# The first expert blocks of a hybrid decoder step: row numbers and first down weights loaded at the end of the output projection

## The reference

```
x  = x + gt1 * (concat([att, conv]) @ w_out)
h2 = rmsnorm(x, g_n2) * (1 + sc2) + sh2
x  = x + gt2 * hierarchical_moe(h2)           # top-1 of 4 groups, top-2 of 8 experts in it

def expert_mlp(xb, w1, w3, w2):               # 32 experts, w1, w3: 1024 x 512, w2: 512 x 1024
    return (silu(xb @ w1) * (xb @ w3)) @ w2
```

## Time and profile before

| what | value |
|---|---|
| median of 3 runs | 2175.88 us (2175.57 to 2178.8) |
| the profiled execution, own time | 2180.36 us |
| its span, first to last instruction | 2178.8 us |
| mean granted TensorE clock | 0.967 of full speed |
| TensorE busy | 1983.6 us, 91% of the span |
| VectorE, ScalarE, GpSimd busy | 72%, 48%, 24% |
| DMA | 553.20 MB, mean 254 GB/s |

### The profile page before, as it was taken

How to read it: one execution, slowest core, us unless ns; L and a number is a source line. 1 busy time by engine, 2 the same in 40 slices (tenths; PEclk the granted TensorE clock), 3 DMA queues, 4 the chain that set the end, 5 groups by cost and what they waited for, 6 DMA issues and landing times. The chain is left out here.

```text
span 2178.8 us, 40353 instructions
## 1 busy us (share of the span) xinstructions
PE 1983.6 (91%) x13272; PEld 1592.3 (73%) x13273; DVE 1563.6 (72%) x3053; ACT 1051.0 (48%) x2056; POOL 533.0 (24%) x571
## 2 busy tenths in 40 slices
PE   5999999998999998699999399999899998999976
PEld 3788888886787786388887378788687876778732
DVE  2648889886888887489997478565447574658757
ACT  2411111111888887244543267555536574557623
POOL 1013444331111153026554201001110101100155
PEclk9999999998999999799999599999999999999989
DMA  8787555665668578767876389974749797769968
GB/s 252 235 279 254 187 190 189 226 227 175 213 177 285 181 280 275 259 196 243 262 278 202 122 300 395 334 289 167 273 173 330 267 359 255 273 234 387 384 238 313
DMA packets 221314, 553.20 MB, mean 254 GB/s; under 512 B 28802, under 2 KB 43482, under 8 KB 219929
## 3 DMA queue, kind: packets, MB, share of 16 engines
q1 hardware_dynamic: 170891, 425.60, 56.1%
q0 software_dynamic: 25088, 75.71, 9.7%
q10 hardware_dynamic: 25239, 50.67, 6.7%
HBM read 456.95 MB, written 167.56 MB: 287 GB/s over the span
## 5 line engine op out<-in xcount | busy, mean ns | idle before, releaser
L2528 DVE TENSOR_TENSOR LO<-WIDE,HI 128x2048 fp32r<-128x2048 f32 x128 | 287.1, 2285 | 86.1 <-ACT HI L2450 86.1
L644 DVE SCALAR_TENSOR_TENSOR arena<-arena,tapw 128x512 f32<-128x512 f32 (+3 forms) x435 | 266.3, 692 | 0.0
L2450 ACT CAST HI<-WIDE 128x2048 fp32r<-128x2048 f32 x128 | 238.0, 1909 | 24.0 <-PEq L217 16.5
L2528 DVE TENSOR_TENSOR LO<-W2E,HI 128x2048 fp32r<-128x2048 f32 x64 | 143.8, 2289 | 92.8 <-ACT HI L2450 92.8
L445 POOL TENSOR_TENSOR STATS<-STATS,K 128x1 f32<-128x1 f32 x16 | 131.3, 8205 | 314.2 <-ACT H L497 314.2
L777 PE MATMUL PJ<-WIN_H,HTH 128*128 128x512 f32 x640 | 160.4, 393 | 5.3 <-ACT HTH L505 4.9
L787 PE MATMUL PJ<-WIN_L,HTH 128*128 128x512 f32 x640 | 158.7, 390 | 0.0
L781 PE MATMUL PJ<-WIN_H,HTL 128*128 128x512 f32 x640 | 158.3, 389 | 0.0
L2450 ACT CAST HI<-W2E 128x2048 fp32r<-128x2048 f32 x64 | 118.8, 1904 | 60.3 <-issue 60.3
L777 PEld LDWEIGHTS PJ<-WIN_H,HTH 128*128 128x128 f32 x640 | 118.6, 188 | 33.5 <-issue 9.0
L781 PEld LDWEIGHTS PJ<-WIN_H,HTL 128*128 128x128 f32 x640 | 120.2, 188 | 25.2
(11 more groups left out here) (366 smaller groups left out, 4500.8 us busy)
## 6 DMA issues: line engine op xcount, KB each, us to landing
WIDE<-in_w_expert_gate SPq DMA_DIRECT2D x64, 1024.0 KB, 8.2
WIDE<-in_w_expert_up SPq DMA_DIRECT2D x64, 1024.0 KB, 10.0
W2E<-in_w_expert_down SPq DMA_DIRECT2D x64, 1024.0 KB, 9.8
expert_rows<-YE ACTq DMA_DIRECT2D x40, 512.0 KB
expert_rows<-NOROWS POOLq DMA_DIRECT2D x11, 1536.0 KB, 11.7
QN<-q_rows SPq DMA_DIRECT2D x48, 256.0 KB
KN<-out_new_k_prompt SPq DMA_DIRECT2D x48, 256.0 KB, 4.9
VN<-out_new_v_prompt SPq DMA_DIRECT2D x48, 256.0 KB, 4.7
```

Of the source, the lines that this page charges most:

```text
L644: ins = nc.vector.scalar_tensor_tensor(out=out, in0=src, scalar=tap, in1=out, op0=ALU.mult, op1=ALU.add)
L2450: nc.scalar.copy(HI[n][:, cols], raw[n][:, cols]).then_inc(hi_ready[n], 1)
L2528: nc.vector.tensor_tensor(LO[n][:, cols], raw[n][:, cols], HI[n][:, cols], ALU.subtract).then_inc(lo_ready[n], 1)
```

## The change

Row numbers: SyncE's program in the output projection gets an end in which it waits for the last write to `slot` and loads the numbers of expert 0's first 32 slots and of the 128 behind them into two columns of a new lasting tile, FIRST_IDX. In the expert stage GpSimd's first two instructions gather XG0 (32 rows) and XG (128 rows) by these columns. The number load for the second small block goes from GpSimd to SyncE, at the start of SyncE's program. GpSimd then gathers that block, waits for the first 128-row block's landing and for its turn (`x_turned` at 2), and enters its loop, which is as it was: it fetches block 0 again. TensorE's first `turn_x` waits for the new gather's semaphore in place of `x_in`. Down weights: expert 0's two halves are loaded by SyncE in round 16 of the output projection; W2E is allotted one stage earlier for that.

```diff
@@ output_projection_and_routing, SyncE
                     if isinstance(i, int) and i == TILES - 1:
                         first_expert("w_expert_up", 1)
+                    if isinstance(i, int) and i == TILES:
+                        w = t["w_expert_down"][0].rearrange("e (k p) d -> e p k d", p=P)[0]
+                        for half in range(2):
+                            ks = slice(half * KF // 2, half * KF // 2 + KF // 2)
+                            sp.dma_start(state["down"][:, ks], w[:, ks]).then_inc(state["down_in"][half], 16)
...
                 sp.wait_ge(h2_out, 16 * ALLT + 16)
+                sp.wait_ge(slot_out, 16 * 2 * ALLT)
+                for n, (at, rows) in enumerate(((0, SMALL_ROWS), (SMALL_ROWS, P))):
+                    sp.dma_start(state["first_rows"][0:rows, n:n + 1], dr["slot"][at:at + rows, :]).then_inc(state["first_rows_in"][n], 16)
@@ experts, SyncE
-                sp.wait_ge(first_x_in, 16)
-                for half in range(2):
-                    sp.dma_start(half_of(W2[:], half), half_of(w2[0], half)).then_inc(w2_in[half], 16)
+                second = nc.s_assert_within(sp.snap(entry(sp, 0, 1, 1, LAST) * CAP), 0, NEXP * CAP - T,
+                                            skip_runtime_bounds_check_because="an expert's blocks stay inside its CAP slots")
+                sp.dma_start(IDXS[:], dr["slot"][ds(second, T), :]).then_inc(second_idx_in, 16)
@@ experts, GpSimd
                     pool.dma_start(IDXS[:], dr["slot"][ds(slot, T), :]).then_inc(sidx_in, 16)
-                    pool.wait_ge(sidx_in, n * 16)
+                    pool.wait_ge(sidx_in, pool.snap(n * 16 - 16))
...
-                second = place(entry(pool, 0, 1, 1, LAST) * CAP, T)
-                pool.dma_start(IDX0[:], dr["slot"][0:T, :]).then_inc(first_idx_in, 16)
-                pool.dma_start(IDXS[:], dr["slot"][ds(second, T), :]).then_inc(sidx_in, 16)
-                pool.wait_ge(first_idx_in, 16)
-                pool.indirect_dma_start(XG0[:], None, dr["h2"], bass.IndirectOffsetOnAxis(ap=IDX0[:].bitcast(U32), axis=0)).then_inc(first_x_in, 16)
-                pool.wait_ge(sidx_in, 16)
+                for n, (rows, dst, come) in enumerate(((T, XG0, first_x_in), (P, XG, first_block_in))):
+                    pool.wait_ge(state["first_rows_in"][n], 16)
+                    pool.indirect_dma_start(dst[:], None, dr["h2"], bass.IndirectOffsetOnAxis(ap=FIRST[0:rows, n:n + 1].bitcast(U32), axis=0)).then_inc(come, 16)
+                pool.wait_ge(second_idx_in, 16)
                 pool.indirect_dma_start(XGS[:], None, dr["h2"], bass.IndirectOffsetOnAxis(ap=IDXS[:].bitcast(U32), axis=0)).then_inc(sx_in, 16)
+                pool.wait_ge(first_block_in, 16)
+                pool.wait_ge(x_turned, 2)
                 with pool.Fori(0, runs(pool)) as g:
@@ experts, TensorE
-                        pe.wait_ge(x_in, 16)
+                        pe.wait_ge(first_block_in, 16)
```

More of the change, by code:

```diff
@@ L192, in decoder_step @@
             state["unit"] = persistent("unit", [P, NEXP])
+            state["first_rows"] = persistent("FIRST_IDX", [P, 16], I32)
+            state["first_rows_in"] = [lasting(f"first_idx_in{n}") for n in range(2)]
+            state["down"] = persistent("W2E", [P, KF, D])
+            state["down_in"] = [lasting(f"down_w_in{half}") for half in range(2)]
             output_projection_and_routing(nc, t, scratch, const, const_at, state)
@@ L197, in decoder_step @@
             state["mods6_in"] = lasting("mods6_in")
-            state["down"] = persistent("W2E", [P, KF, D])
             state["x6_in"] = [lasting(f"x6_early_in{n}") for n in range(3)]
@@ L2290, in experts @@
         w1_in, w3_in = state["first_in"]
-        w2_in = [sem(f"down_w_in{half}") for half in range(2)]
+        w2_in = state["down_in"]
         idx_in, x_in = sem("idx_in"), sem("xg_in")
@@ L2298, in experts @@
                                         "y_taken", "y_out"))
-        first_idx_in, first_x_in, first_turned = sem("first_idx_in"), sem("first_x_in"), sem("first_turned")
+        first_x_in, first_block_in, first_turned, second_idx_in = sem("first_x_in"), sem("first_block_in"), sem("first_turned"), sem("second_idx_in")
         table = state["blocks"]
         SEL, BASE = sb("SEL", [P, ALLT * 2, NEXP]), sb("BASE", [P, ALLT * 2])
-        IDXS, IDX0, XG0 = sb("IDXS", [T, 1], I32), sb("IDXS0", [T, 1], I32), sb("XGS0", [T, D])
+        IDXS, XG0 = sb("IDXS", [T, 1], I32), sb("XGS0", [T, D])
+        FIRST = state["first_rows"]
         step = sem("dest_step")
```

## The result

The changed kernel takes 2190.78 us (2190.47 to 2195.31, 4 runs) against 2177.34 (2175.57 to 2178.95) for the kernel before: a ratio of 1.0068, 95% interval 1.0053 to 1.0082, 13.4 us slower. The forecast was 2181 with a range of 2174.5 to 2187.

What follows compares the result with a forecast made beforehand. TensorE was taken to bound the expert loop; the first big matmul gains 8.0 us, but the second block's rows come 2.9 us late plus 2.0 of clock: 2175.9 + 4.9 = 2180.8, written 2181, range 2174.5 to 2187.

Steps and rivals of the forecast that it cites:

- The end of the output projection: SyncE's added loads before the stage's closing barrier: cost 0, hidden under GpSimd's drain, bounded by 0 and 1 us.
- the small block's gain: First small block at the expert stage's entry: rows 3 us sooner, of which ScalarE's four casts leave 0.8 us.
- The stop at the second block: TensorE waits about 11 us for the second 128-row block's rows, some 12 us behind its first big matmul.
- The sum is +2.9 + 2.0 = +4.9 us: At the second 128-row block: 2.9 us lost by late rows plus 2.0 us for TensorE's fallen clock.
- The third term: GpSimd's chain ahead of the second block: block 0's gather to landing 5.5 us, then 3.5 to the next number load.
- The step that failed: Expert loop: bound by TensorE, so a stall inside it moves the end by as much.
- The fourth rival: Row chain stays the bound in the loop: fetch cycle over TensorE's, further stalls, 2185 to 2192 us; chance 0.08.
- the upper bound of the forecast's sum, +13.5: Second block with all chain terms near the top: 11.0 us late plus 2.5 of clock, called unlikely.
- Quiet queues: Rival: both index loads and gathers run at least times, second block on time, 2174.5 to 2178 us; chance 0.33.
- The rule of about 2.0 us and the bytes by 436 GB/s: Rival from the skill page for GpSimd DMAs: chain at least times, no net change; same chance as quiet queues, 0.33.
- The faster case: Rival: chain from first turn to second block's rows under 17.4 us keeps the eight us, 2168 to 2171.5; chance 0.06.
- The output projection's end: Rival: SyncE's loads or the 2 MB delay the closing barrier, adding 1 to 3 us; chance 0.03.

Runs made afterwards that it cites:

- E9: The changed kernel, two waits and refetch kept, with the third small block's row numbers loaded early by SyncE: 2184.46 us, ratio 1.0038 to the kernel before.
- E8: The changed kernel with block 0 fetched once, both waits kept, and the third small block's numbers loaded early by SyncE: 2173.28 us, ratio 0.9987 to the kernel before.
- E1: The changed kernel with block 0 fetched once and neither wait ahead of GpSimd's loop: 2170.74 us, ratio 0.9970 to the kernel before.
- E5: The changed kernel with block 0 fetched once but both waits kept ahead of GpSimd's loop: 2179.38 us, ratio 0.9999 to the kernel before.
- E11: The kernel before with only the down weights and the third small block's numbers loaded early: 2170.22 us, ratio 0.9968 to the kernel before.

## Why the prediction was wrong

The direction, the mechanism and the first place were right; the size was not, for two reasons: terms of the first stop were mis-sized, and a second stop was put at nothing.

**What held.** The end of the output projection cost nothing: SyncE was ready before GpSimd's drain was over, and the drain was again 3742 ns. ScalarE's four casts left little of the small block's gain. Block 0 was to be turned 15.1 us behind the first cast, and was at 15.6; the first big matmul was to start at 20.9, and did at 21.2. The stop at the second block came where and why it was forecast, and the clock fell behind it: from block 1's turn to its first product 9.5 us (1271.25 to 1280.77) for 7.3 before, 2.2 us where I had 2.0. The rule of the Trainium skill in "TensorE: Matmul & The Clock Gate", "HAM oscillation", that a wait for a DMA between groups of matmuls puts the array back to its low clock, agrees with the trace: behind the wait of 13.63 us the granted clock was 0.51 from 1271 to 1277, so the stop cost more than its length.

**The terms of the chain that were mis-sized.** "The sum is +2.9 + 2.0 = +4.9 us" was 6.0 + 2.2 = 8.2 at that place. From block 0's turn to block 1's rows I had 28.4 us and it took 30.9:

| term | forecast | measured |
|---|---|---|
| table reads | 4.9 | 5.6 (1240.3 to 1245.86) |
| numbers of block 0 | 5.3 | 5.6 (to 1251.43) |
| gather of block 0, and on to the next numbers | 5.5 + 3.5 | 12.4 (to 1263.78) |
| numbers of block 1 | 4.6 | 3.1 (to 1266.93) |
| gather of block 1 | 4.6 | 4.3 (to 1271.25) |

The third term carries it: the gather took 2.70 us to issue and some 8.9 to land, near the most of the earlier trace rows (9.2), and I had taken 5.5, under the median. The next down weights were asked for at the same time (1251.20), and from 1254 to 1262 the DMA engines were busy throughout (a share of 1.01). From 1264 to 1268 they were idle (0.01), and there the numbers of block 1 were quick. The other 0.5 us of the 6.0 is a TensorE that was that much later at block 0.

**The step that failed.** The sum ended at block 1: "whatever ... stalls it inside the loop, moves the end by as much" was taken to mean that nothing more would follow. Measured, another 6.0 us followed at block 6 (4.73 of waiting, the rest the clock). The fourth rival ("the second stall is followed by more: 2185 to 2192", chance 0.08) had the time, 2190.78 us, but not the cause: it asked for a fetch cycle longer than TensorE's, and its sum of 17.6 against 18.2 seemed to rule that out. The cycle was mis-sized too: in the changed kernel the gathers from 1277.77 to 1332.89 follow each other by 18.3, 18.3 and 18.5 us. That is over TensorE's by 0.6 us in all, far from 4.73. What was missing is that a cycle of equal length is enough: a late chain keeps its lateness unseen until something is added to it, and the small block at the end of a run adds an index load and a gather. The trace of the kernel before had the sign of it, with 0.7 us to spare at that place. E9 took one index load out and the 6 us went; in E8's profile the stop of 6.88 us went as well. With both stops as measured the sum is 8.2 + 6.0 = 14.2, against 14.0 from the first cast to the end in the profiles and 13.4 in the times. That the upper bound of the forecast's sum, +13.5, lies beside the measured 13.4 is luck: it had all of it at the second block.

**The rivals.** Quiet queues was wrong: of the four transfers two were quick and two were near the slow end. The rule of about 2.0 us and the bytes by 436 GB/s for a GpSimd DMA ("DMA: Bandwidth & Descriptors", "Anatomy of one DMA", the Trainium skill) comes near the load of block 1's numbers in idle queues, which landed after 2.3 us. For the 512 KB of a gather it would give about 3.2 us, an estimate from that page's figures: 4.3 were measured in nearly idle queues and 8.9 under weight loads. The faster case needs its condition met, and E1 does it by taking out the cause: 2170.74 us. The output projection's end did not come later.

## What to carry to other kernels

When a prefetch is put ahead of a loop, the loop's first iteration has to be taken out with it; a fetch repeated "for free" is a whole cycle of a serial chain, and a wait that protects its buffer puts the chain's table reads and transfers in the open. If the fetching engine's cycle is about as long as the computing engine's, lateness is not won back until the computing engine has something extra to do (in E5 the gather at 1390.24, behind the second stop and the small block, waits 17.24 us for TensorE again). See for each gather whether it waits for the consumer (the chain is in time) or for its own numbers (it may be late), read from its landing how much is to spare, and look for the place where the next extra transfer stands. Count starts from a point of the stage itself when the stages ahead scatter by more than the change.

## What was unexpected of the hardware

- The same indirect gather of 128 rows took 0.97 us to issue in one place and 2.70 in another of the same kernel, and 4.3 or 8.9 us to land. The slow one ran beside weight loads (a DMA share of 1.01 from 1254 to 1262), the quick one behind a stretch with none (0.01 from 1264 to 1268).
- The wait for 128 row numbers came in two sizes, 2.6 and 5 to 6 us behind the load's issue, in one stretch of one kernel (E5: 2.56, then 5.14, 5.12, 5.14 and 6.02).
- GpSimd's drain ahead of the barrier took 3742 ns to the nanosecond in both kernels, and 3742 or 3745 ns in every experiment.
- Moving two loads of 1 MB alone (E4) brought no gain and a scatter of 12 us between executions, with a stop that came in one profile and not in the other. The kernel before scattered by 9.0 us (26 executions) and 8.0 (23) on the same chips, E11 by 7.4 (8), so how much of the 12 is the stop's is open.
